# Row pitches of 2080 and 4160 bytes for the activation chunks and the split weights of an fp32 transformer stack on one core

## The reference

```python
x = x + mixed @ w_out                                   # after h @ w_in, attention, an S5 scan, y @ w_glu
ff = (silu(h2 @ w_ff_gate) * (h2 @ w_ff_up)) @ w_ff_down   # 2048 x 5632, 5632 x 2048
...
for layer in range(2):                                  # second block
    mix = gmlp_shortconv_mixer(...) if layer % 2 == 0 else dilated_attention_mixer(...)
    h = h + rmsnorm(mix, norm_mix_post[layer])
    f = square(relu(rmsnorm(h) @ w_up)) @ w_down        # 2048 x 8192, 8192 x 2048
    h = h + rmsnorm(f, norm_mlp_post[layer])
```

## The kernel before

| tile | first byte in the partition | pitch of its rows | first byte of a row, modulo 512 |
|---|---|---|---|
| KPA | 32896 | 2048 | 128 for every row |
| HI | 90240 | 4096 | 128 for every row and both column halves |
| LO | 102528 | 4096 | 128, the same |
| KPB | 134912 | 2048 | 256 for every row |

## Time and profile before

### The profile page before, as it was taken

One profiled execution on the slowest core, in us unless ns is written; L12 is line 12 of the kernel. 1 busy time (PEld: TensorE's weight loads), 2 busy tenths in 40 slices (PEclk: granted clock), 3 DMA queues, 4 the chain that ended last, 5 costly groups with the idle time before them and its releaser, 6 DMA issues. The chain is left out here.

```text
span 3386.3 us, 38632 instructions
## 1 busy us (share of the span) xinstructions
PE 3273.7 (97%) x15842; PEld 2670.4 (79%) x15842; DVE 1866.3 (55%) x1958; ACT 1475.8 (44%) x1760; POOL 119.8 (4%) x99
## 2 busy tenths in 40 slices
PE   6988999999999999999999999999999999999998
PEld 5776788888888778878888888878787788888886
DVE  6455655555555544665555555565555655555555
ACT  5434444444444444444444444444444544444443
POOL 4230000000000000000000000000000000000000
PEclk9998999999999999999999999999999999999999
DMA  7233455555555555555555555545454555555554
GB/s 200 93 119 121 159 187 186 188 188 193 189 186 187 181 172 188 194 174 180 191 188 190 186 187 186 185 156 186 149 174 154 173 184 186 187 187 187 187 188 146
DMA packets 187548, 596.28 MB, mean 176 GB/s; under 512 B 12491, under 2 KB 19308, under 8 KB 186860
## 3 DMA queue, kind: packets, MB, share of 16 engines
q1 hardware_dynamic: 187372, 593.82, 53.9%
HBM read 588.54 MB, written 5.23 MB: 175 GB/s over the span
## 5 line engine op out<-in xcount | busy, mean ns | idle before, releaser
L1063 DVE TENSOR_TENSOR LO<-RAW,HI 128x1024 fp32r<-128x1024 f32 (+1 forms) x1104 | 1351.6, 1226 | 1183.2 <-ACT HI L576 1181.4
L576 ACT ACTIVATE HI<-RAW 128x1024 fp32r<-128x1024 f32 (+1 forms) x1104 | 1159.2, 1052 | 1396.5 <-PE PS L1884 1392.1
L1884 PE MATMUL PS<-HI,KPA 128*128 128x512 f32 x5376 | 1499.4, 395 | 18.0 <-issue 5.3
L1884 PEld LDWEIGHTS PS<-HI,KPA 128*128 128x128 f32 x5376 | 1008.5, 190 | 233.4 <-issue 15.8
L1884 PE MATMUL PS<-HI,KPB 128*128 128x512 f32 x3392 | 954.9, 397 | 3.9 <-DVE ACC L1559 3.3
L1884 PE MATMUL PS<-LO,KPA 128*128 128x512 f32 x2688 | 841.4, 394 | 9.9 <-DVE LO L1063 9.8
L1884 PEld LDWEIGHTS PS<-HI,KPB 128*128 128x128 f32 x3392 | 631.6, 188 | 150.5 <-issue 5.2
L1884 PEld LDWEIGHTS PS<-LO,KPA 128*128 128x128 f32 x2688 | 509.0, 190 | 122.2 <-DVE LO L1063 11.9
L1884 PE MATMUL PS<-LO,KPB 128*128 128x512 f32 x1696 | 533.9, 395 | 0.8 <-DVE KPB L1099 0.8
L1884 PEld LDWEIGHTS PS<-LO,KPB 128*128 128x128 f32 x1696 | 318.8, 188 | 77.5 <-issue 1.2
L603 ACT ACTIVATE KPB<-PS 128x512 fp32r<-128x512 f32 x98 | 58.6, 599 | 185.0 <-PE PS L1909 185.0
(11 more groups left out here) (255 smaller groups left out, 988.2 us busy)
## 6 DMA issues: line engine op xcount, KB each, us to landing
RAW<-in_w_up SPq DMA_DIRECT2D x128, 1024.0 KB, 5.1
RAW<-in_w_down SPq DMA_DIRECT2D x128, 1024.0 KB, 5.5
RAW<-in_w_qkv SPq DMA_DIRECT2D x48, 1024.0 KB, 5.1
RAW<-in_w_ff_gate SPq DMA_DIRECT2D x88, 512.0 KB, 3.7
RAW<-in_w_ff_up SPq DMA_DIRECT2D x88, 512.0 KB, 4.6
RAW<-in_w_ff_down SPq DMA_DIRECT2D x44, 1024.0 KB, 5.5
RAW<-in_w_in_ab SPq DMA_DIRECT2D x40, 1024.0 KB, 5.0
RAW<-in_w_in SPq DMA_DIRECT2D x16, 1024.0 KB, 6.2
```

Of the source, the lines that this page charges most:

```text
L576: e.activation(HI[:, s % NSPLIT, 0:w], RAW[:, d % NRAW, j, 0:w], ACT.Copy).then_inc(S("hi_made"), 1)
L1063: e.tensor_tensor(LO[:, h, 0:w], RAW[:, d % NRAW, j, 0:w], HI[:, h, 0:w].bitcast(F32), ALU.subtract).then_inc(S("lo_made"), 1)
L1884: ins = e.matmul(PS[:, b + j, 0:cw], l, r[:, h, 512 * j:512 * j + cw], start=(i == 0 and part == 0), stop=(last and part == 2))
```

## The change

The rows of `KPA` and `KPB` become 520 numbers long (2080 bytes) and those of `HI` and `LO` 1040 numbers (4160 bytes); only the first 512 and 1024 of each are used. The tiles grow by 1408 bytes in all, for which there was no room; so the region that is kept free at the bottom of the partition shrinks from 16384 to 4096 bytes (`dynamic_dma_scratch_size`), and every tile moves down. Nothing else changes: each engine's list of instructions and waits is the same, row for row, but for line numbers, which are 6 higher.

```diff
-SBUF_FROM = 16512
+SCRATCH = 4096
+SBUF_FROM = SCRATCH + 128
...
+    def rows(t, width):
+
+        return t[:, :, 0:width]
+
     XR = sb("XR", [128, 2, D])
     kpa_at = at[0]
-    KPA = sb("KPA", [128, 16, 2, 256], F32R)
+    KPA = rows(sb("KPA", [128, 16, 520], F32R), 512).rearrange("p k (a c) -> p k a c", a=2)
     RAW = sb("RAW", [128, NRAW, 2, 1024])
-    HI = sb("HI", [128, NSPLIT, 1024], F32R)
-    LO = sb("LO", [128, NSPLIT, 1024], F32R)
+    HI = rows(sb("HI", [128, NSPLIT, 1040], F32R), 1024)
+    LO = rows(sb("LO", [128, NSPLIT, 1040], F32R), 1024)
     ACC = sb("ACC", [128, 2, D])
...
-    ph_at = at[0] + 32768
+    ph_at = at[0] + 33280
     BLT = sb("BLT", [128, 4, 2, 8, 128], where=kb)
-    KPB = nc.alloc_sbuf_tensor_at("KPB", [128, 16, 2, 256], F32R, offset=at[0])
+    KPB = nc.alloc_sbuf_tensor_at("KPB", [128, 16, 520], F32R, offset=at[0])
+    KPB = rows(KPB, 512).rearrange("p k (a c) -> p k a c", a=2)
...
-    acc_at = kpa_at + 32768 + 24576 + 24576
+    acc_at = kpa_at + 33280 + 24576 + 24960
...
-    nc = _bacc.Bacc("TRN2", target_bir_lowering=False, num_devices=1)
+    nc = _bacc.Bacc("TRN2", target_bir_lowering=False, num_devices=1, dynamic_dma_scratch_size=SCRATCH)
```

## The result

The changed kernel takes 3418.77 us (median of 4 runs, 3416.83 to 3420.82) against 3388.14 us before: +30.6 us, a ratio of 1.0091 with the interval 1.0074 to 1.0109. It is slower, by two and a half times the forecast +12.3 us, and inside the stated range of 3340 to 3440 us, but above 3392 to 3415 us, which the prediction called the forecast's own range.

What follows compares the result with a forecast made beforehand. TensorE's matmul stream was taken to bound the kernel; +25.0 us on KPA and -12.7 us on KPB gave +12.3 us, so 3400 us against the 3388 median. The range was 3340 to 3440, the forecast's own 3392 to 3415.

Steps and rivals of the forecast that it cites:

- What bounds the kernel: TensorE's stream of 13152 matmuls, busy 3273.7 of 3386.3 us; their pace counts, with almost no time spent waiting.
- The mechanism: On TensorE, weight load and moving-data stream collide depending on their offsets, holding 13.4 ns a matmul on KPA, 20.0 on KPB.
- The other engines, the writers, the DMAs at nothing: VectorE, ScalarE, KPB row writers and RAW loads were given no cost; 13 us was the writers' upper bound.
- a third of the way from the first middle to the second: New pace for all matmuls, 230.5 ns, between the middles of settled (230.0) and unsettled (231.6) paces.
- The upper middle of the prediction: Middle of the two unsettled matmul paces, 231.0 on KPA and 232.3 on KPB: 231.6 ns.
- The present averages: Mean matmul paces before the change: 227.4 ns on KPA (an estimate) and 233.0 ns on KPB.
- The term for KPA: Loss on matmuls with weights in KPA: 8064 x (230.5 - 227.4) = +25.0 us.
- that for KPB: Gain on matmuls with weights in KPB: 5088 x (230.5 - 233.0) = -12.7 us.
- The rival of no change: KPA's loss and KPB's gain cancel, or a coarser property such as partition half matters: 3388 us within 0.2%; chance 0.18.
- The faster rival: Most new offset pairs collide less; all matmuls at KPA's settled pace save 37.7 us, giving 3350; chance 0.34.
- Its extreme end: Collisions vanish and every matmul takes 213.3 ns, saving 214 us: 3174; over 50 us faster had chance 0.06.
- The clearly slower rival: All matmuls at KPB's pace or worse, as odd multiples of 32 bytes are less aligned: +49.1 us, 3437; chance 0.10.

Runs made afterwards that it cites:

- e1: Kernel before with KPB moved from 256 to 128 modulo 512, where KPA, HI and LO begin: 3355.62 us, ratio 0.9914.
- e2: Kernel before with KPA at 256 and KPB at 384 modulo 512, HI and LO staying at 128: 3396.23 us.
- e8: Kernel before with KPA, KPB, HI and LO all beginning at 256 modulo 512, pitches as before: 3354.43 us.
- e9: Kernel before with pitches of 2304 (KPA, KPB) and 4352 bytes (HI, LO), all tiles at 128 modulo 256: 3357.42 us, ratio 0.9918.
- e3: Kernel before with the 2080-byte pitch for KPA and KPB alone, KPB beginning at 128 modulo 512: 3413.49 us, ratio 1.0083.
- e6: Kernel before with KPA 32 and KPB 96 bytes past HI and LO modulo 256, pitches as before: 3436.94 us.
- e5: Kernel before with KPA 64 and KPB 192 bytes past HI and LO modulo 256, pitches as before: 3407.99 us.
- e7: Kernel before with KPA 160 and KPB 224 bytes past HI and LO modulo 256, pitches as before: 3429.95 us.
- e11: Kernel before with KPA, KPB and HI at 128 modulo 256 and LO at 192, pitches as before: 3395.00 us, ratio 1.0028.

## Why the prediction held in direction and missed in size

**What bounds the kernel**: right. The same waits, nearly the same idle time (33.5 against 32.6 us), and the difference lies in the pace of line 1890.

**The mechanism**: right, and shown by more than the change itself. The pace depends on the offset between the weight load and the moving operand (e1, e2, e8, e9). I had it modulo 512; it is modulo 256 (e2, the chunks k and k + 8 in e3, and e9, whose rows alternate modulo 512). Two rivals for the other side of the offset can be looked up. ScalarE and VectorE write HI and LO at the same offsets as TensorE reads them; but from 1500 us on, matmuls on KPA whose gap fell mostly where neither of the two worked stand 226.7 ns apart before (475 gaps) and 233.5 in e6 (632 gaps), so the difference is there without them. RAW, where the DMAs write, begins at KPA's own offset modulo 256 in every run with the old pitches, while KPA's pace goes from 226.7 to 233.3. That the two reads collide was argued, not shown: no view shows a read waiting. What is shown is that the excess depends on their distance at full clock, and that it isn't there at half clock: in all twelve traces the gaps at half clock (400 to 450 ns, 76 to 104 of them in each) have a mean of 425 to 426 ns.

**The other engines, the writers, the DMAs at nothing**: right; the means of the other engines' instructions are the same to the nanosecond, and the loads of the last layers' "up" weights land in 5.1 us as before.

**The size**: the step that failed is "I take 230.5 for all, a third of the way from the first middle to the second". The measured pace is 232.3 on KPA and 232.2 on KPB. The four paces that the trace of before held came from two of eight distances, and one of them, distance 0, is the best of all; a middle between it and its neighbour stood for six distances of which five are at 233.3 or above. The upper middle of the prediction, 231.6, called unsettled, would have been closer, but not for its reason: the eight settled paces average 232.0, so that what I called unsettled is worth only the last 0.3 ns. The present averages were good: over all gaps at full clock the trace of before has 227.4 and 233.0 (the working given for the first, one in seven or eight at 231.0, comes to 227.2 or 227.3). The term for KPA was set at 3.1 ns a matmul and is 4.9 (232.3 - 227.4), that for KPB at -2.5 and is -0.8 (232.2 - 233.0).

With these the sum would be 8064 x 4.9 - 5088 x 0.8 = 39.5 - 4.1 = +35.4 us, more than the measured 30.6. The first part of the kernel gives some back. These are the windows 0 to 335 us for the matmuls of the line alone (us, busy and count on PE and PEld), of the kernel after:

```profile
0.00:335.00 335.00, 181.16 (x662) 130.13 (x663) 0.92 0.45 134
```

and of the kernel before:

```profile
0.00:335.00 335.00, 178.94 (x662) 129.88 (x663) 0.93 0.46 134
```

Both have issued 662 of them by then: TensorE waits for some 60 us in this stretch (it is busy with all its matmuls for 274.43 of the 335 us before, and 275.97 after), and a slower matmul takes its time out of a wait. They are all on KPA, so 662 x 4.9 = 3.2 us are hidden; that leaves 32.2. The two traces, set side by side matmul by matmul, agree: the starts at 335 us lie 0.02 us apart, and behind that the gaps at full clock grow by 35.9 us on KPA and shrink by 3.7 us on KPB. Another 3.7 us come back, nearly all of them in gaps of 300 ns and more, which leaves the 28.5 us by which the spans differ. The medians differ by 2.1 us more than these two executions, which is within the spread of the runs.

**The rival of no change** fell: the mean over the offsets lies 2.7 ns above the weighted pace of before (232.3 against 229.6), and its other ground, a coarser property, falls with e1 against e6: the pace of the same matmuls on KPB goes from 226.9 to 234.2 ns with the offset alone. The rule of the Trainium skill ("SBUF — State Buffer", section "Who interferes with whom") that TensorE's two read ports are independent does not describe this; the measurement decides. **The faster rival** fell with e5 to e7: its idea that distances of a multiple of 128 might be the worst is wrong at 0, the best. Its extreme end was reached by none of the eight; nor was the 215.8 ns of the prediction, from a formula that the Trainium skill ("TensorE: Matmul & The Clock Gate", section "Back-to-back issue gap") gives for the gap of a single isolated matmul, not for a stream of weight loads and matmuls as here. Its other number, 3350 us with all matmuls at 226.7 ns, is nearly what e1 gave (3355.6) by 384 bytes ahead of KPB. **The clearly slower rival**, all at KPB's pace or worse, is what five of the eight distances are; that 0 and 192 are among the eight kept the time from its 3437 us. Its reason, that odd multiples of 32 are less aligned, isn't borne out: distance 64 is as slow as 32, 160 and 224.

## What to carry to other kernels

Where matmuls of 512 fp32r columns stream at full clock, each with a weight load of its own, the offset in the partition between stationary and moving operand, modulo 256 bytes, was worth up to 7.5 ns on a matmul here (3.3%); put every row of both at the same offset modulo 256, padding included, and look at the pace tile by tile in the timeline, since two tiles with the same instructions and another pace are the sign of it. Before spreading addresses so as to average a collision out, find out whether the present relation is a good or a bad one: an average is a gain only over a relation that is worse than the average. When two values bound an unknown, ask how many others there are that the trace has never visited.

## What the runs showed that I had not expected

The pace isn't a smooth function of the distance: 0 gives 226.7 ns, 192 gives 228.9, and the other six lie between 232.3 and 234.2. Two moving tiles that no matmul reads together (HI and LO, e11) cost 2.6 ns a matmul over their own shares when they stand 64 bytes apart. ScalarE and VectorE write rows of KPB that begin at odd multiples of 32 bytes in the same mean time as when all began at 256 modulo 512 (599 and 692 ns, before and after). At distance 0 the settled starts seem to keep step with something outside of the stream: in e1's trace those with a gap of 226 or 227 ns on both sides (10804 of them) all lie at one phase of a period of 6.667 ns, within the resolution of 1 ns, from the first to the last and across every interruption, and 34 such periods are the gap of 226.7. What it is, no run isolates. Distances between multiples of 32 were not tried, nor matmuls without their weight loads, so that whether it is the weight load's read that holds up the moving stream, or the other way round, stays open.
